# A hybrid decoder layer on one core: expert weights reloaded in two steps, and the final norm moved into the experts' block

## The reference, cut to what matters

```python
u = rmsnorm(x, norm_ffn_w) * (1 + sc2) + sh2
y = moe(u, ...)          # 64 experts, top 8 per token, blocks of 128 rows, plus a shared expert
x = x + gt2 * y
...
return rmsnorm(x, final_norm_w)
```

## Time and profile before

| | us |
|---|---|
| median of 3 runs | 2970.38 (2961.32 to 2972.79) |
| time of the profiled execution | 2965.84 |
| its span in the profile | 2964.0 |
| PE busy, whole span | 2788.4 (94%) |
| DVE / ACT / POOL busy | 1065.2 / 574.3 / 795.5 |

### The profile page before, as it was taken

The page is one execution under the profiler, slowest core; times in us unless marked ns, Lnnn a source line. Parts: engine busy times, 40 slices in busy tenths (PEclk is TensorE's granted clock), DMA queues, the critical chain, the costliest instruction groups (busy, mean ns, idle before and its releaser), DMA issues. The chain is left out here.

```text
span 2964.0 us, 31405 instructions
## 1 busy us (share of the span) xinstructions
PE 2788.4 (94%) x10377; PEld 1651.8 (56%) x10378; DVE 1065.2 (36%) x1644; ACT 574.3 (19%) x1072; POOL 795.5 (27%) x1000
## 2 busy tenths in 40 slices
PE   7998999998899799999999898999999999999993
PEld 4555888874566556666666566444444444444442
DVE  3333323314775388842111273322222212222224
ACT  3213333314343100011000230111111111111112
POOL 2000122202342000000000013655556555565540
PEclk8998999989899799999999999999999999999996
DMA  6520000101011211211302120787776888887863
GB/s 234 229 85 24 15 22 15 51 18 43 15 29 24 60 32 32 61 32 34 101 22 74 74 102 30 255 276 253 253 218 212 284 283 279 283 264 250 282 183 124
DMA packets 162806, 382.24 MB, mean 129 GB/s; under 512 B 24595, under 2 KB 111711, under 8 KB 134793
## 3 DMA queue, kind: packets, MB, share of 16 engines
q1 hardware_dynamic: 130449, 311.52, 29.3%
q0 software_dynamic: 32256, 69.33, 10.0%
HBM read 339.65 MB, written 72.94 MB: 139 GB/s over the span
## 5 line engine op out<-in xcount | busy, mean ns | idle before, releaser
L2508 PE MATMUL ps<-big 128*128 x1536 | 679.3, 595 | 13.4 <-SPq L2435 12.6
L2508 PEld LDWEIGHTS ps<-big 128*128 128x128 f32 x1536 | 285.5, 191 | 339.1 <-issue 339.0
L2461 POOL DMA_INDIRECT big<-u_rows,big x384 | 392.9, 1023 | 170.3 <-issue 89.0
L1707 PE MATMUL ps<-big 128*128 128x352 f32 x1152 | 347.7, 462 | 11.3 <-DMA big<-in_w_branch 11.3
L2518 PE MATMUL ps<-big 128*128 x768 | 345.8, 593 | 3.7 <-ACT big L2571 3.7
L1707 PEld LDWEIGHTS ps<-big 128*128 128x128 f32 x1152 | 220.1, 191 | 135.6 <-DMA big<-in_w_branch 12.2
L2518 PEld LDWEIGHTS ps<-big 128*128 128x128 f32 x768 | 145.4, 190 | 188.8 <-issue 188.8
L2611 DVE SCALAR_TENSOR_TENSOR big<-big,ps 128x256 f32<-128x256 f32 x96 | 64.0, 667 | 491.7 <-ACT big L2561 469.4
L842 PE MATMUL ps<-big 128*128 128x352 f32 x576 | 207.5, 467 | 1.9 <-DMA big<-in_w_in 1.9
L1266 PE MATMUL ps<-big 128*128 128x352 f32 x576 | 183.0, 468 | 5.4 <-DVE big L1481 2.7
L2477 POOL DMA_INDIRECT y_rows<-big x96 | 155.8, 1623 | 110.0 <-issue 60.6
(11 more groups left out here) (549 smaller groups left out, 3086.2 us busy)
## 6 DMA issues: line engine op xcount, KB each, us to landing
big<-in_exp_w_gate SPq DMA_DIRECT2D x64, 1024.0 KB
big<-in_exp_w_up SPq DMA_DIRECT2D x64, 1024.0 KB
big<-in_exp_w_down SPq DMA_DIRECT2D x64, 1024.0 KB
big<-in_ada_w SPq DMA_DIRECT2D x24, 1024.0 KB, 8.3
big<-in_w_in SPq DMA_DIRECT2D x48, 512.0 KB, 4.2
big<-in_w_in SPq DMA_DIRECT2D x6, 1024.0 KB, 5.2
big<-in_w_branch SPq DMA_DIRECT2D x24, 256.0 KB, 4.5
big<-u_rows,big POOLq DMA_INDIRECT x384
```

Source lines behind the costliest of these rows:

```text
L1707: ins = pe.matmul(ps[:, c, 0:CW], ring_g[:, q % 2, j, :], k.hT[:, j, c * CW:(c + 1) * CW], start=(j == 0), stop=(j == KT - 1))
L2461: g.indirect_dma_start(out=x_rows[:, u, x * 256:(x + 1) * 256], out_offset=None, in_=u_quarters, in_offset=bass.IndirectOffsetOnAxis(idx_i ...
L2508: ins = pe.matmul(ps[:, 2 + u, :].rearrange("p (g f) -> p g f", f=FF), xT[:, u, j, :], gate_up[:, j], start=(j == 0), stop=(j == KT - 1))
```

## The change

Three things change. SP's reload of a slot is split: gate and up are issued when the last up product of the slot's old expert is done, and down when its last down product is done. The two conditional ranges are nested, so that one jump passes both. And `finish` is no longer a block of its own: each engine's part follows its part of the experts, with a new semaphore `all_added` from POOL to SP. Within the finish, the spreads go from POOL to DVE (gate rows) and ACT (norm row); the root's table is called up early by a one-element `Sqrt`; tiles 1 to 8 are multiplied by the gate row on POOL and only tile 0 on DVE; and the norm's row stays in PSUM banks 4 and 5, where the final product reads it.

```diff
+    f = Finish(k)
     def over_ranges(eng, run):
         total = eng.value_load(k.end_tab[0:1, E_N - 1:E_N], min_val=1, max_val=NBLK)
         run(*RANGES[0])
-        for first, last in RANGES[1:]:
-            with eng.If(total > first):
-                run(first, last)
+        with eng.If(total > RANGES[1][0]):
+            run(*RANGES[1])
+            with eng.If(total > RANGES[2][0]):
+                run(*RANGES[2])
...
+            def reload(e, s, blocks_before):
+                wait_before_addressed(sp, up_done, blocks_before, sp_passed)
+                load_part(k, sp, e, s, 0)
+                load_part(k, sp, e, s, 1)
+                wait_before_addressed(sp, down_done, blocks_before, sp_passed)
+                load_part(k, sp, e, s, 2)
...
-                    wait_before_addressed(sp, down_done, before, sp_passed)
-                    load(i * NW + (NW + s), s)
+                    reload(i * NW + (NW + s), s, before)
...
+            finish_sync(k, f, sp)
...
             over_ranges(g, run)
+            finish_gpsimd(k, f, g)
...
+def finish_sync(k, f, sp):
+    a = k.a
+    sp.wait_ge(f.all_added, 1)
+    for t in range(NT):
+        n = tokens_of(t)
+        sp.dma_start(f.rows[0:n, t, :], k.y_rows[t * P:t * P + n, :]).then_inc(f.loaded[t], 16)
...
+def finish_gpsimd(k, f, g):
+    g.sem_inc(f.all_added, 1)
+    for t in range(1, NT):
+        n = tokens_of(t)
+        g.wait_ge(f.loaded[t], 16)
+        g.wait_ge(f.rows_ready, 1 if t < 8 else 2)
+        g.tensor_tensor(f.rows[0:n, t, :], f.rows[0:n, t, :], f.rows_of[0:n, t // 8, :], ALU.mult).then_inc(f.gated, 1)
...
+def finish_scalar(k, f, act):
...
+    act.activation(f.spread[2][:, :, :], bcast(k.prm[:, c0:c0 + KT].unsqueeze(2), KT, P), ACT.Copy).then_inc(f.norm_spread, 1)
+    act.wait_ge(f.eps_ready, 1)
+    act.activation(f.warm[:, :], f.eps[:, :], ACT.Sqrt)
+    for x in range(2):
...
+def finish_vector(k, f, v):
...
+    v.tensor_copy(f.spread[0][:, :, :], bcast(k.mod[:, 5 * KT:6 * KT, 0:1], KT, P)).then_inc(f.gate_spread, 1)
...
+        v.scalar_tensor_tensor(f.out[0:n, t % 3, :].rearrange("p (b c) -> p b c", b=2), f.rows[0:n, t, :].rearrange("p (b c) -> p b c", b=2),
+                               f.total[0:n, t:t + 1], ps[0:n, NORM_BANK:NORM_BANK + 2, :], ALU.mult, ALU.mult).then_inc(f.finished, 1)
+
+    for t in range(NT):
+        n = tokens_of(t)
+        if t == 0:
+            v.wait_ge(f.loaded[0], 16)
+            v.wait_ge(f.rows_ready, 1)
+            st(v.tensor_tensor(f.rows[:, 0, :], f.rows[:, 0, :], f.rows_of[:, 0, :], ALU.mult))
+        else:
+            v.wait_ge(f.gated, t)
+        v.wait_ge(f.turned, t + 1)
+        r = f.rows[0:n, t, :].rearrange("p (b c) -> p b c", b=2)
+        v.tensor_tensor(r, r, ps[0:n, banks_of(t):banks_of(t) + 2, :], ALU.add).then_inc(f.summed, 1)
+        if t == 1:
+            v.wait_ge(f.spread_turned, 3)
+        if t:
+            normalise(t - 1)
+    normalise(NT - 1)
```

More of the change, by code:

```diff
@@ L2442, in _ @@
                 before = sp.value_load(k.end_tab[0:1, e - NW:e - NW + 1], min_val=1, max_val=NBLK)
-                wait_before_addressed(sp, down_done, before, sp_passed)
-                load(e, e % NW)
+                reload(e, e % NW, before)
             sp.wait_ge(weights_loaded[(E_N - 1) % NW], ((E_N - 1) // NW + 1) * 48)
             sp.sem_inc(weights_ready, 1)
+            finish_sync(k, f, sp)
         @block.gpsimd
@@ L2555, in _ @@
             over_ranges(pe, run)
+            finish_tensor(k, f, pe)
         @block.scalar
@@ L2597, in _ @@
             over_ranges(act, run)
+            finish_scalar(k, f, act)
         @block.vector
@@ L2646, in _ @@
             over_ranges(v, run)
+            finish_vector(k, f, v)
 def add_shared(v, k, st):
@@ L2657, in add_shared @@
     st(v.tensor_tensor(xs, xs, ys, ALU.add))
[L2660 to L2758, removed]
@@ new lines, with __init__ @@
+class Finish:
+    def __init__(self, k):
+        w, late = Area(k.big[:, 0:MOE]), Area(k.ring)
+        self.rows = w.take(NT, D)
+        self.out, self.squares, self.rows_of = late.take(3, D), late.take(2, D), late.take(2, D)
+        self.spread = [late.take(KT, P), late.take(KT, NS), late.take(KT, P)]
+        self.total, self.eps, self.warm = late.take(NT), late.take(1), late.take(1)
+        self.loaded, self.stored = [k.sem(f"fi_loaded{t}") for t in range(NT)], [k.sem(f"fi_stored{u}") for u in range(3)]
+        (self.all_added, self.gate_spread, self.norm_spread, self.spread_turned, self.rows_ready, self.gated, self.turned, self.summed,
+         self.scaled, self.rooted, self.finished, self.eps_ready, self.dstep) = (
+            k.sem("fi_" + x) for x in ("all_added", "gate_spread", "norm_spread", "spread_turned", "rows_ready", "gated", "turned",
+                                       "summed", "scaled", "rooted", "finished", "eps_ready", "dve_step"))
@@ new lines, in finish_sync @@
+def finish_sync(k, f, sp):
[5 more added lines that the diff above has]
+    for t in range(NT):
+        sp.wait_ge(f.finished, t + 1)
+        if t < 8:
+            sp.dma_start(a["y_prompt"][0, t * P:(t + 1) * P, :], f.out[:, t % 3, :]).then_inc(f.stored[t % 3], 16)
+        else:
+            sp.dma_start(a["y_sample"].rearrange("s l d -> (s l) d"), f.out[0:NS, t % 3, :]).then_inc(f.stored[t % 3], 16)
+    for u in range(3):
+        sp.wait_ge(f.stored[u], 16 * (NT // 3))
@@ new lines, in finish_gpsimd, with banks_of, finish_tensor @@
+def finish_gpsimd(k, f, g):
[5 more added lines that the diff above has]
+        g.tensor_tensor(f.rows[0:n, t, :], f.rows[0:n, t, :], f.rows_of[0:n, t // 8, :], ALU.mult).then_inc(f.gated, 1)
+NORM_BANK = 4
+def banks_of(t):
+    return 6 if t % 2 == 0 else 0
+def finish_tensor(k, f, pe):
+    ps = k.ps
+    for x in range(3):
+        n = NS if x == 1 else P
+        if x < 2:
+            pe.wait_ge(f.gate_spread, x + 1)
+        else:
+            pe.wait_ge(f.norm_spread, 1)
+        for j in range(KT):
+            ins = pe.transpose(ps[0:n, 2 * x + j // 4, (j % 4) * P:(j % 4 + 1) * P], f.spread[x][:, j, :], k.ident[:, :])
+        ins.then_inc(f.spread_turned, 1)
+    for t in range(NT):
+        n = tokens_of(t)
+        if t == 1:
+            pe.wait_ge(f.rows_ready, 1)
+        if t >= 2:
+            pe.wait_ge(f.summed, t - 1)
+        for j in range(KT):
+            ins = pe.transpose(ps[0:n, banks_of(t) + j // 4, (j % 4) * P:(j % 4 + 1) * P], k.xT[:, j, t * P:t * P + n], k.ident[:, :])
+        ins.then_inc(f.turned, 1)
@@ new lines, in finish_scalar @@
+def finish_scalar(k, f, act):
+    ps = k.ps
+    c0 = PRM["final_norm_w"]
+    act.activation(f.spread[2][:, :, :], bcast(k.prm[:, c0:c0 + KT].unsqueeze(2), KT, P), ACT.Copy).then_inc(f.norm_spread, 1)
+    act.wait_ge(f.eps_ready, 1)
+    act.activation(f.warm[:, :], f.eps[:, :], ACT.Sqrt)
+    for x in range(2):
+        n = NS if x == 1 else P
+        act.wait_ge(f.spread_turned, x + 1)
+        act.activation(f.rows_of[0:n, x, :].rearrange("p (b c) -> p b c", b=2), ps[0:n, 2 * x:2 * x + 2, :], ACT.Copy)\
+           .then_inc(f.rows_ready, 1)
+    for t in range(NT):
+        n = tokens_of(t)
+        act.wait_ge(f.summed, t + 1)
+        act.activation(f.squares[0:n, t % 2, :], f.rows[0:n, t, :], ACT.Square, accum_out=f.total[0:n, t:t + 1]).then_inc(f.scaled, 1)
+        act.wait_ge(f.scaled, t + 1)
+        act.activation(f.total[0:n, t:t + 1], f.total[0:n, t:t + 1], ACT.Sqrt, scale=1.0 / D, bias=f.eps[0:n, :]).then_inc(f.rooted, 1)
@@ new lines, in finish_vector, with normalise @@
+def finish_vector(k, f, v):
+    ps = k.ps
+    st = Steps(v, f.dstep)
+    v.tensor_copy(f.spread[0][:, :, :], bcast(k.mod[:, 5 * KT:6 * KT, 0:1], KT, P)).then_inc(f.gate_spread, 1)
+    v.tensor_copy(f.spread[1].rearrange("p k (s l) -> p k s l", l=SL),
+                  bcast(k.mod[:, 5 * KT:6 * KT, 1:NSEQ].unsqueeze(3), KT, SB, SL)).then_inc(f.gate_spread, 1)
+    v.memset(f.eps[:, :], EPS).then_inc(f.eps_ready, 1)
+    def normalise(t):
+        n = tokens_of(t)
+        v.wait_ge(f.rooted, t + 1)
+        st(v.reciprocal(f.total[0:n, t:t + 1], f.total[0:n, t:t + 1]))
+        if t >= 3:
+            v.wait_ge(f.stored[t % 3], 16 * (t // 3))
+        v.scalar_tensor_tensor(f.out[0:n, t % 3, :].rearrange("p (b c) -> p b c", b=2), f.rows[0:n, t, :].rearrange("p (b c) -> p b c", b=2),
+                               f.total[0:n, t:t + 1], ps[0:n, NORM_BANK:NORM_BANK + 2, :], ALU.mult, ALU.mult).then_inc(f.finished, 1)
+    for t in range(NT):
+        n = tokens_of(t)
+        if t == 0:
+            v.wait_ge(f.loaded[0], 16)
+            v.wait_ge(f.rows_ready, 1)
+            st(v.tensor_tensor(f.rows[:, 0, :], f.rows[:, 0, :], f.rows_of[:, 0, :], ALU.mult))
+        else:
+            v.wait_ge(f.gated, t)
+        v.wait_ge(f.turned, t + 1)
+        r = f.rows[0:n, t, :].rearrange("p (b c) -> p b c", b=2)
+        v.tensor_tensor(r, r, ps[0:n, banks_of(t):banks_of(t) + 2, :], ALU.add).then_inc(f.summed, 1)
```

(6 more changed lines are left out.)

## The result

The changed kernel takes 2930.05 us (median of 4 runs, 2925.23 to 2939.07); the kernel before, run beside it, 2965.85 (2961.25 to 2972.79). The ratio is 0.9879 with a 95% interval of 0.9858 to 0.99: faster by 36 us, 1.2%. Forecast were 2948 us, 22.4 us off, and a range that ended at 2935. The direction was right and the gain was 1.6 times the forecast, outside the range.

What follows compares the result with a forecast made beforehand. PE was taken as nearly always busy in the experts, with the chain of adds into y_rows binding behind it. Terms 1 + 9.5 + 11.9 = 22.4 us off 2970.4 gave 2948 us, range 2935 to 2958.

Steps and rivals of the forecast that it cites:

- The reload: SP's split weight loads in the experts: up to 16.2 us of PE's time, but the adds decide, so 1 us taken.
- bound on the adds' pace: Adds from block 48 to 88: earlier loads raise the DMA share, 0.05 us an add; nothing taken, 3 us either way.
- Rival 1: In the experts, the adds keep up with PE and the weights' waits count in full: 2933 us, chance 0.10.
- Rival 2: Between blocks 41 and 88 earlier loads collide with the adds; at 1.2 us an add 2996 us; chance 0.06.
- The joint: From experts to finish: one jump and no drain, so SP's loads of y_rows start 9.5 us earlier.
- Rival 4: At the experts' end, the drain is work POOL must do anyway: 2952 to 2955 us, chance 0.12.
- The tiles: In the finish, DVE sets the pace at 2.53 us a tile, POOL's product takes 2.38: 11.9 us saved.
- Rival 3: In the finish POOL and DVE take turns, a tile costs up to 3.7 us: 2958 us, chance 0.10.
- the norm's row in PSUM: In the finish, DVE's final product reading this row from PSUM was costed at nothing.

Runs made afterwards that it cites:

- reload_only: The kernel before with only SP's split reload; ranges, barrier and finish stay as they were: 2953.7 us, ratio 0.9946.
- two_ifs: The changed kernel with the two conditional ranges side by side again instead of nested: 2931.7 us.
- norm_sbuf: The changed kernel with the norm's weight row copied to SBUF by ACT, from where DVE's final product reads it: 2935.2 us.
- early_unsplit: The changed kernel with the down part issued right behind gate and up, into unused SBUF, so the load has no gap: 2945.5 us, ratio 0.9935.

## Why the prediction was wrong

**The step that failed** is in "The reload": "the adds decide. If PE comes 10.9 us earlier (7.3 + 3.6) at block 48, add 48 still follows add 47's landing, and each later one its predecessor", with 1 us taken for the whole reload. It measured 14 to 16 us. Its first half was right: the adds are a chain, and with it slower or the loads in one piece PE waits for ACT in place of SP (27.6 us and 11.7 us). What failed is that I held the chain's length fixed. From add 0 to add 95 it took 1015.2 us in the kernel before and 998.6 in the changed one. The copies were also not as close to late as I had them: at block 48 the lag was 32.2 us where PE first waits at 40.

**The bound on the adds' pace** failed with it. I took an add's cost as proportional to the mean DMA share, and the share did not fall: from 2400 to 2820 us it is 0.85 against 0.83 in the kernel before, at a pace of 10.85 against 11.03. The same bytes, issued at other times, changed the pace by 0.2 to 0.3 us a block; I had allowed 3 us either way, which over 40 blocks is 0.08 each, a third of that. The faster pace shows in the other kernels with the split reload too (10.87 us in `reload_only`, 10.86 in `two_ifs`, 10.75 in `norm_sbuf`). That the order matters for the time is shown by `early_unsplit` against the changed kernel. Why the adds land sooner stays open. A pause between the parts cannot be the whole of it, since `early_unsplit` has none and has the same pace from block 16 on; an early start alone cannot either, since that kernel is slower. The spacing of its adds there is also the changed kernel's: from 8.9 us, with a median of 10.5, to over 13, against a median of 11.1 in the kernel before.

**Rival 1**, the weights' waits in full, gave 2933 us with a chance of 0.10; that is the case that came, and my range stopped 2 us short of it. The evidence that I set against it, a pace of 11.03 and a wait of 9.95 us, was measured under the old traffic. **Rival 2**, loads that collide with the adds, may be what slowed the first 16 blocks of `early_unsplit`; there it ate the gain and no more.

**The joint** was forecast at 9.5 us and measured 11.1. Jump and issue took 2.7 us as taken (2.9). The rest, 1.5 us, is the last add's landing: 2.7 us from issue to branch, where it was 4.2. **Rival 4** is out: POOL's products followed the loads with no trace of the 6.55 us, which stayed in `reload_only`, where the barrier stayed. **The tiles** came at 2.52 us against 2.53, POOL's product at 2.36 against 2.38, and 11.5 us against 11.9. **Rival 3** is out for the changed kernel, and in `norm_sbuf` it is real. That the norm's row in PSUM costs nothing was right as a price, and too little as a reading: it saves some 5 us beside POOL's products.

## What to carry to other kernels

A chain that seems to bind behind the bound engine has a length that was measured under the present traffic. Set its events beside those of the bound engine, block by block, to see how much room is left; one long wait of a third engine does not tell. When the change moves that traffic, its order too, its pace is a term of its own and wants a wide range, in both directions. Two waits that a transfer can be split between are worth trying even where the first part gains little by being early: 1 MB early and 2 MB late gave all that 2 and 1 did. And before work goes to POOL beside DVE, count the SBUF tensors of DVE's instructions: with one of them in PSUM, DVE's product kept the 1.28 us that it has without POOL beside it.

## What the runs showed of the hardware

An unchanged stream of bytes, its first two thirds issued up to 14 us earlier, let indirect DMAs with an add through at 10.85 us a block and not 11.03 to 11.16 (blocks 48 to 88), with the last third issued later or at once. After a jump over a long stretch of code POOL took 2.5 to 3.0 us to its next instruction, PE up to 7.5 us, ACT and DVE under 0.7. POOL's drain at the end of the experts' block took 6546 ns in both kernels that had one, although its last DMA had landed 5.6 us before it began.
